# Two of the projections' tile pairs go from direct products to seven-product slots, and the mixer's pieces are placed anew

## The reference

```python
xn   = rmsnorm(x, norm1_g)
q, k, v, r, a_lr, cb, cc, ch, cu, cv = split(xn @ w_in)    # 512, 512, 1024, 1024, 16, then five of 512
loga = log_sigmoid(a_lr @ w_a2 + b_a) / 16
o, S = gla_chunked(q, k, v, loga, S0)                      # gated linear attention, chunks of 64
o_gla  = rmsnorm_per_head(o) * gla_g * silu(r)
o_conv = cb * (conv_b + sum_j conv_w[j] * shifted(cc * ch, j))
vv     = layernorm(gelu(cv));  o_cm = gelu(cu) * (Wm @ vv + cm_bs)     # ChunkMLP, chunks of 128
h = x + concat[o_gla, o_conv, o_cm] @ w_out
y = rmsnorm(h + swiglu(rmsnorm(h, norm2_g)), final_g)
```

## Time and profile before

| | before |
|---|---|
| three runs | 2188.55, 2187.94, 2188.02 us; median 2188.02 |
| the profiled execution's own time | 2187.62 us |
| its span in the trace | 2185.9 us |
| PE busy | 2173.7 us, 99%, 17352 matmuls |
| DVE, ACT, POOL busy | 1714.6 (78%), 1003.4 (46%), 9.0 us (0%) |
| granted TensorE clock, mean | 0.997 |

### The profile page before, as it was taken

One profiled execution on the slowest core, in us unless ns is written; L12 is line 12 of the kernel. 1 busy time (PEld: TensorE's weight loads), 2 busy tenths in 40 slices (PEclk: granted clock), 3 DMA queues, 4 the chain that ended last, 5 costly groups with the idle time before them and its releaser, 6 DMA issues.

```text
span 2185.9 us, 40925 instructions
## 1 busy us (share of the span) xinstructions
PE 2173.7 (99%) x17352; PEld 2168.9 (99%) x17352; DVE 1714.6 (78%) x1994; ACT 1003.4 (46%) x1331; POOL 9.0 (0%) x14
## 2 busy tenths in 40 slices
PE   9999999999999999999999999999999999999998
PEld 9999999999999999999999999999999999999998
DVE  7765478446796789888888887888888888787887
ACT  7433523124454455444444544444444545444455
POOL 0000000000000000000000000000000000000000
PEclk9999999999999999999999999999999999999998
DMA  5332324245333435344445445434545876555523
GB/s 191 95 109 89 106 69 146 80 143 195 110 107 106 149 116 166 123 150 160 141 141 158 145 128 165 152 124 146 163 141 174 302 279 225 181 208 190 188 84 115
DMA packets 121583, 325.63 MB, mean 149 GB/s; under 512 B 10702, under 2 KB 51214, under 8 KB 120432
## 3 DMA queue, kind: packets, MB, share of 16 engines
q1 hardware_dynamic: 120928, 323.82, 44.0%
q10 hardware_dynamic: 528, 0.07, 0.0%
HBM read 267.22 MB, written 56.63 MB: 148 GB/s over the span
## 4 chain that ended last, share of the span: by engine, by line
PE 97%; DVE 1%; issue 1%; ACT 1%; POOL 0%; POOLq 0%; DVEq 0%; ACTq 0%
PE acc L1622 24%; PE acc L1307 21%; PE g L1622 18%; PE acc L1630 12%; PE g L1630 9%; PE acc L1531 2%; PE acc L1569 2%; PE g L1531 2%; PE g L1569 2%; PE g L1523 1%; PE acc L1523 1%; PE g L1334 0%; PE g L1457 0%; PE g L1326 0%; PE g L1464 0%
## 5 line engine op out<-in xcount | busy, mean ns | idle before, releaser
L1128 ACT CAST w_hi<-w_s 128x1024 fp32r<-128x1024 f32 (+1 forms) x204 | 209.1, 1025 | 357.1 <-DVE w_s L2438 351.0
L1622 PE MATMUL g<-op_hi,w_hi 128*128 128x272 f32 x1056 | 272.1, 288 | 0.0
L1622 PE MATMUL acc<-op_hi,w_hi 128*128 128x272 f32 x1056 | 271.7, 288 | 0.4 <-ACT acc L1102 0.4
L1622 PE MATMUL g<-op_lo,w_hi 128*128 128x272 f32 x1056 | 271.9, 288 | 0.0
L1622 PE MATMUL acc<-sg_hi,w_hi 128*128 128x272 f32 x1056 | 271.8, 288 | 0.0
L1622 PE MATMUL acc<-op_lo,w_hi 128*128 128x272 f32 x1056 | 271.4, 288 | 0.0
L1622 PE MATMUL acc<-sg_lo,w_hi 128*128 128x272 f32 x1056 | 271.4, 288 | 0.0
L1307 PE MATMUL acc<-op_hi,w_hi 128*128 128x272 f32 x1280 | 267.6, 290 | 0.0
L1307 PE MATMUL acc<-op_hi,w_lo 128*128 128x272 f32 x1280 | 264.8, 288 | 0.0
L1307 PE MATMUL acc<-op_lo,w_hi 128*128 128x272 f32 x1280 | 264.7, 288 | 0.0
L2413 DVE TENSOR_TENSOR w_lo<-w_s,w_hi 128x1024 fp32r<-128x1024 f32 (+1 forms) x204 | 242.7, 1190 | 12.4 <-ACT w_hi L1128 6.4
(11 more groups left out here) (396 smaller groups left out, 4676.8 us busy)
## 6 DMA issues: line engine op xcount, KB each, us to landing
w<-w_gu SPq DMA_DIRECT2D x88, 512.0 KB, 3.3
w_raw<-w_gu SPq DMA_DIRECT2D x88, 512.0 KB, 3.9
w_raw<-w_in SPq DMA_DIRECT2D x64, 512.0 KB, 3.6
hf_dram<-hf_hi SPq DMA_DIRECT2D x22, 952.0 KB, 6.4
hf_dram<-hf_lo SPq DMA_DIRECT2D x22, 952.0 KB, 8.7
w_raw<-w_d SPq DMA_DIRECT2D x32, 512.0 KB, 4.3
w<-w_d SPq DMA_DIRECT2D x26, 512.0 KB, 3.2
op_hi<-hf_dram SPq DMA_DIRECT2D x16, 544.0 KB, 7.0
```

Of the source, the lines that this page charges most:

```text
L1128: nc.scalar.copy(w_hi[:, (C_ST + n) % RING, 0:w], src[:, 0:w]).then_inc(hi_ready, 1)
L1622: nc.tensor.matmul(out, w_h, x, start=fresh and j == 0 and i == 0, stop=False, skip_group_check=True)
```

## The change

Four of r's eight tiles (those of the attention's `mix` tiles 4 to 7) leave the stage of half tiles. Their columns of w_in go in front of those of k and v, and are made in two slots more (`NR = 2`, `NQ = 8`), with seven products each, ahead of k. Their outputs lie in `trunk` 12 to 15 until SP stores them to `r_dram` (two stores of 0.56 MB), since v needs the place. Late in the stage they are read back (one DMA of 1.11 MB), ACT takes their Silu at `C_T` + 37, and DVE multiplies them into `mix` at the next chunk.

The stage has 48 half tiles instead of 56, and all pieces are placed anew. From `C_T`: vt 0, 1, 2; z 3, 6; b 5, 7, 9, 11, 13; kdt 15; qs 17 to 24; mu 18; var_cm 20; s 22, 25, 27, 29, 31, 32, 33, 35, 36, 37; vvt 25; zc 26, 27; p 28, 30, 32, 34; on 35, 37, 39, 41. The heads are normed in the order 2, 3, 0, 1. w_out's seven-product half now takes `mix` tiles 4 to 11, and its direct half 12 to 15 and 0 to 3. The square root and DVE's reciprocal in the answers to var_cm and on become Ln and Exp(-0.5 ·) on ACT. The reload of x for tiles 12 to 15 moves to the stage's last chunk.

```diff
-T_Q, T_CV, T_CONV, T_CU, T_R, N_IN = 1, 17, 21, 33, 37, 45
+T_Q, T_CV, T_CONV, T_CU, T_R, N_IN = 1, 17, 21, 33, 37, 41
-NQ = 6
+NR = 2
+NQ = NR + 6
-MIX_ORDER = list(range(HK, KT)) + list(range(HK))
+MIX_ORDER = list(range(4, 12)) + list(range(12, KT)) + list(range(4))
+HEAD_ORDER = (2, 3, 0, 1)
-B_AT = tuple(C_T + 8 + 2 * i for i in range(5))
-KDT_AT = C_T + 18
-QS_AT = tuple(C_T + 20 + i for i in range(8))
-MU_AT, VAR_CM_AT, VVT_AT, ZC_AT = C_T + 19, C_T + 21, C_T + 28, (C_T + 30, C_T + 32)
-S_AT = (C_T + 25, C_T + 29, C_T + 32) + tuple(C_T + 33 + 2 * i for i in range(7))
-P_AT = tuple(C_T + 34 + 2 * i for i in range(4))
-OSQ_AT = C_T + 40
-ON_AT = tuple(C_T + 42 + 2 * i for i in range(4))
+B_AT = tuple(C_T + 5 + 2 * i for i in range(5))
+KDT_AT = C_T + 15
+QS_AT = tuple(C_T + 17 + i for i in range(8))
+MU_AT, VAR_CM_AT, VVT_AT, ZC_AT = C_T + 18, C_T + 20, C_T + 25, (C_T + 26, C_T + 27)
+S_AT = tuple(C_T + i for i in (22, 25, 27, 29, 31, 32, 33, 35, 36, 37))
+P_AT = tuple(C_T + 28 + 2 * i for i in range(4))
+OSQ_AT = C_T + 34
+ON_AT = tuple(C_T + 35 + 2 * i for i in range(4))
+R_AT = C_T + 37
...
+        def slot_out(s):
+            return kv[:, s + 4 if s < NR else s - NR]
...
             for s in range(1, NQ):
                 for j in (1, 3, 0, 4, 2):
                     load_kv_block(s, j)
+                if 2 <= s < NR + 2:
+                    sp.wait_ge(kv_out, s - 1)
+                    sp.wait_ge(kv_read, 4 * (s - 1))
+                    sp.dma_start(r_dram[:, 2 * (s - 2):2 * (s - 1), :], slot_out(s - 2)).then_inc(r_out, 16)
...
-                if c == C_T + 10:
+                if c == C_T + 13:
                     sp.wait_ge(inter, number(("z", 1)))
                     load_s0(0)
                     load_s0(1)
...
-                    for i in range(4):
+                    for i in range(3):
                         sp.dma_start(trunk[:, 4 * i:4 * i + 4, :], xT[:, 4 * i:4 * i + 4, :]).then_inc(x_back, 16)
+                if c == P_AT[-1] + 8:
+                    sp.wait_ge(inter, number(("p", PAIRS - 1)))
+                    sp.wait_ge(r_out, 16 * NR)
+                    sp.dma_start(trunk[:, KT - 2 * NR:, :], r_dram).then_inc(r_in, 16)
+                if c == C_OUT - 1:
+                    sp.wait_ge(front_done, 2 * NR)
+                    sp.dma_start(trunk[:, 12:, :], xT[:, 12:, :]).then_inc(x_back, 16)
...
-                    last = nc.scalar.activation(two(orstd), g01[:, :, 0:TH], ACT.Sqrt, bias=EPS, scale=1.0 / DV)
+                    chain(nc.scalar.activation(two(orstd), g01[:, :, 0:TH], ACT.Ln, bias=EPS, scale=1.0 / DV))
+                    last = nc.scalar.activation(orstd, orstd, ACT.Exp, scale=-0.5)
...
                 split_hi(c + 4, c + 4)
+                if c == R_AT:
+                    act.wait_ge(r_in, 16)
+                    for i in range(2 * NR):
+                        nc.scalar.activation(trunk[:, KT - 2 * NR + i, :], trunk[:, KT - 2 * NR + i, :], ACT.Silu)\
+                            .then_inc(r_act, 1)
...
-                    chain(nc.vector.reciprocal(orstd, orstd))
                     if i < 3:
                         out_square_sum(i + 1)
                     for e in range(2):
-                        m = 2 * i + e
+                        m = 2 * HEAD_ORDER[i] + e
...
                 split_lo(c + 4, c + 4)
+                if c == R_AT + 1:
+                    dve.wait_ge(post_v, parts(V_KINDS, ("on", 1)))
+                    for i in range(2 * NR):
+                        dve.wait_ge(r_act, i + 1)
+                        nc.vector.tensor_tensor(mix[:, 4 + i, :], mix[:, 4 + i, :], trunk[:, KT - 2 * NR + i, :],
+                                                ALU.mult).then_inc(front_done, 1)
...
-    kv = np.concatenate([wk, wv], axis=1)
+    kv = np.concatenate([wr[:, (KT // 2 - 2 * NR) * P:], wk, wv], axis=1)
```

More of the change, by code:

```diff
@@ L268, in build @@
         form_lo = (sg_lo[:, 0], opf_lo[:, 0], opf_lo[:, 1], sg_lo[:, 1], opf_lo[:, 2], sg_lo[:, 2], opf_lo[:, 3])
-        mg = mxf[:, HK * T:].rearrange("p (i b t) -> p i b t", i=HP, b=4)
+        mg = mxf[:, 4 * T:12 * T].rearrange("p (i b t) -> p i b t", i=HP, b=4)
         ta_hi, ta_lo = ([o[:, f // 2, HP * (f % 2):HP * (f % 2) + HP] for f in range(4)] for o in (opf_hi, opf_lo))
@@ L272, in build @@
         mixform_lo = (fa_lo[:, 0], ta_lo[0], ta_lo[1], fa_lo[:, 1], ta_lo[2], fa_lo[:, 2], ta_lo[3])
-        kv = trunk[:, 4:KT, :].rearrange("p (s m) t -> p s m t", s=NQ)
+        kv = trunk[:, 4:KT, :].rearrange("p (s m) t -> p s m t", s=NQ - NR)
         y_out = [[y[:, f, 0:HP, :] for f in range(4)] for y in (y_first, y_second)]
         aside = hid.rearrange("p (q r) t -> p q r t", q=2)
+        r_dram = nc.dram_tensor("r_dram", (P, 2 * NR, T), F32).ap()
         h_dram = nc.dram_tensor("h_dram", (P, KT, T), F32).ap()
@@ L325, in build @@
         x_back = sem("x_back")
+        r_out = sem("r_out")
+        r_in = sem("r_in")
+        r_act = sem("r_act")
+        front_done = sem("front_done")
         wa_in = sem("wa_in")
@@ L672, in _ @@
             spill_h(7)
-            sp.wait_ge(mix_done, 8)
+            sp.wait_ge(mix_done, 4)
             sp.dma_start(conv_o, cst[:]).then_inc(stored, 16)
@@ L843, in out_squares @@
                 for e in range(2):
-                    nc.scalar.activation(osq[:, e, :], mix[:, 2 * h + e, :], ACT.Square).then_inc(osq_a, 1)
+                    nc.scalar.activation(osq[:, e, :], mix[:, 2 * HEAD_ORDER[h] + e, :], ACT.Square).then_inc(osq_a, 1)
             def post(kind, i):
@@ L882, in post @@
                 elif kind == "var_cm":
-                    last = nc.scalar.activation(two(lnb[:]), g23[:, :, 0:TH], ACT.Sqrt, bias=EPS, scale=1.0 / (4 * P))
+                    chain(nc.scalar.activation(two(lnb[:]), g23[:, :, 0:TH], ACT.Ln, bias=EPS, scale=1.0 / (4 * P)))
+                    last = nc.scalar.activation(lnb[:], lnb[:], ACT.Exp, scale=-0.5)
                 elif kind == "vvt":
@@ L913, in op_hi_tile @@
             def op_hi_tile(k):
-                act.wait_ge(mix_done, k + 1)
+                act.wait_ge(mix_done, k - 3)
                 act.wait_ge(chunk_done, C_OUT)
@@ L918, in mix_single_hi @@
             def mix_single_hi():
-                act.wait_ge(mix_done, 8)
+                act.wait_ge(mix_done, 4)
+                act.wait_ge(front_done, 2 * NR)
                 act.wait_ge(post_v, parts(V_KINDS, order[-1]))
@@ L951, in mix_block_hi @@
                     else:
-                        act.wait_ge(mix_done, KT)
+                        act.wait_ge(mix_done, KT - 2 * NR)
                     nc.scalar.copy(aside[:, :, 1, :], pc[:, :, 0:TH]).then_inc(p5_aside, 1)
@@ L1980, in post @@
                     dve.wait_ge(post_a, parts(A_KINDS, (kind, i)))
-                    chain(nc.vector.reciprocal(lnb[:], lnb[:]))
                     for h in range(4):
@@ L2184, in kv_outputs @@
             def kv_outputs(s, piece):
-                q, y = s % 2, kv[:, s]
+                q, y = s % 2, slot_out(s)
                 dve.wait_ge(chunk_done, done_q(NPQ * s + (5, 5, 6, 7)[piece]))
                 if piece == C11:
+                    if s >= NR + 4:
+                        dve.wait_ge(r_out, 16 * (s - NR - 3))
                     nc.vector.tensor_tensor(y[:, 0, 0:TH], pa[:, q, 0:TH], rstd[:, 0:TH], ALU.mult).then_inc(kv_read, 1)
@@ L2746 @@
     conv = np.concatenate([y[:, i * P:(i + 1) * P] for i in range(4) for y in (wcc, wch, wcb)], axis=1)
-    win = tiles(np.concatenate([wq, wcv, conv, wcu, wr], axis=1))
+    win = tiles(np.concatenate([wq, wcv, conv, wcu, wr[:, :(KT // 2 - 2 * NR) * P]], axis=1))
     wo = a["w_out"][0].reshape(KT, P, D)[MIX_ORDER].reshape(D, D)
```

## The result

The changed kernel took 2207.94 us in the median of five runs (2205.84 to 2210.51), against 2187.98 of the kernel before in runs beside it (2187.76 to 2188.55). The ratio is 1.0091, with a 95% interval of 1.008 to 1.0102. It is slower by 20 us, where 11.4 were forecast. The profiled execution took 2205.84 us, the fastest of the five, so its trace has 18.2 us to explain, and the median has 2 more.

The account below looks back on a forecast made before the run. PE's in-order queue was taken to bound the kernel from end to end. Waits of 16.3 us, less an old wait of 0.3 and saved work of 4.6, gave +11.4: 2199.0 profiled, 2199.4 median; range 2194.5 to 2206.

Parts of the forecast that it names:

- Work saved, 4.6 us: PE's matmul work: eight half tiles go (48.16 us), two seven-product slots come (43.54), saving 4.6 us.
- The waits of the stage, 1 to 7: PE waits at z1 3.8, mu 0.9, s1 2.0, p1 0.9, s5 2.0, on0 3.6, on3 0.8 us.
- z1's: Wait 1: PE waits ahead of z1 for DVE's and ACT's answer to b0, 3.8 us.
- 6: Wait 6: on0 behind s7 in one half tile, PE waits for DVE's updates, 3.6 us.
- Wait 8, w_out's start, 2.3 us: PE waits at w_out's first products because DVE builds their forms 2.4 us later than before; 2.3 us.
- PE's clock falls in the waits: Rival: granted clock halves after long waits, 2.7 us per fall; 2202.1 for one, 2204.8 for two; chance 0.22.
- the two longest waits: Waits 1 and 6: z1 behind b0, 3.8 us, and on0 behind s7, 3.6 us.
- the rival's 2204.8: Clock rival's time in us if the clock falls in both of the two longest waits; rival's chance 0.22.
- DMA lateness: Rival: S0's first loads or r's read-back late, lateness beyond 15 us paid one for one; 2203 and over; chance 0.06.
- one load for Ln and Exp: Rival: ACT's answers to `on` are one 1.28 us table load shorter; 2197.5 us; chance 0.08.
- hidden answers: Rival: answers reach PE in time, only saved work shows; 2183.4 us; chances 0.04 faster, 0.05 same.
- these eight waits: Forecast waits 1 to 7 in the stage and 8 at w_out's start, 16.3 us in sum.

Follow-up runs that it names:

- the last kernel: Changed kernel with all freed waits, pieces moved earlier, ACT answering on1 to on3 before the Silu, x reloads behind late weight blocks; 2183.01 us, ratio 0.9977 to the kernel before.
- the kernel with four long waits: The changed kernel itself, with the waits at z1, s1, s5 and on0; 2207.94 us, ratio 1.0091 to the kernel before.
- the two with one: Kernel before with b0 ahead of z1, 2192.88 us; changed kernel with z1, on0, mu, p1 and s5 waits freed, 2195.68 us.
- the one with everything freed: Changed kernel with freed waits, x reloads spread, and kdt, qs, mu, var_cm, s0, vvt one half tile earlier; 2188.91 us, ratio 1.0004 to the kernel before.

## Why the prediction was wrong

- *Work saved, 4.6 us*: right. It is the 43.6 and 48.0 of the account to within 0.2, and what the last kernel gains.
- *The waits of the stage, 1 to 7*: right, each within 0.4 us, 13.8 for 14.0 in sum. (By its own rows, 6 is 3.5 and not 3.6.) z1's, freed alone, was paid back in full, and of the 9.9 us of five freed together 1.4 came back as a new wait and 0.6 at w_out.
- *Wait 8, w_out's start, 2.3 us*: mis-sized; it is 3.4 by the list and 3.9 by the starts. The bound for it reached only from zero to 1 us more. The mechanism (forms late by DVE's and ACT's queues behind on3) was right: with the on answer ahead of the Silu 2.3 us of it go, and with the stage's other lateness too, all of it. Spreading the reloads of x alone gave nothing; with ACT's new order the block behind them does hold ACT, for 5.2 us, and how much moving them to the end adds in the last kernel wasn't tried by itself.
- *"PE's clock falls in the waits", 0.22*: this is the step that failed. It wasn't a rival to the count but a part of it. I priced a fall at 2.7 us and allowed it in the two longest waits; a stretch at 0.50 costs 1.53, but it comes behind the waits of 2.0 and 1.8 us too. The profiled execution lost 4.6 us so, behind z1, s1 and s5. That the rival's 2204.8 lies within 1.1 of the profiled 2205.84 is partly luck: two falls at 2.7 are nearly as much as three at 1.53, and behind on0, one of the two that it named, the clock didn't fall in this execution. The granted clock of its five runs (0.993 to 0.995, the slowest run at 0.993) against 0.997 for the kernel before puts the median's further 2 us there as well; the trace of a slower run isn't at hand, so that is argued and not shown. The scatter speaks for it, though not alone: 4.7 us over the five runs of the kernel with four long waits, 1.6 and 2.1 in the two with one, 0.8 over ten runs in the last kernel with none; but 2.9 in the one with everything freed, whose waits in the stage and in w_out are of 1.6 us at most.
- *DMA lateness, one load for Ln and Exp, hidden answers*: none of the three happened in the changed kernel; no wait of PE's list ends with a DMA.
- Forecast of +11.4 and found +18.2 in the profile, 6.8 more: 4.6 are the clock, 1.6 w_out's start, and 0.6 small differences of the other terms. The direction and the place were right, the range ended 2 us too low.

## What to carry to other kernels

When the busiest engine runs in order and is fed by answers, compressing the schedule is not free even if every engine has room: write down, for each pair of neighbouring pieces, what the second really waits for. Five of these eight waits weren't asked for by the data: one was for a bank where another was free, four were for answers that the piece, or its first matmuls, didn't use. The cure was another bank, a shorter list, another order in the half tile, or a wait moved behind the matmuls that don't need it. With them freed, a few pieces moved, ACT's order turned round and the reloads of x put at the end, a change that lost 20 us gains 5. Price a stall of TensorE of 2 us and more at its length plus a part of the clock's fall, and read the windows behind every such wait, and the scatter of the runs.

## What the runs showed of the hardware

In eight profiles (the changed kernel and seven experiments) there were 24 waits of PE of 1.8 to 3.4 us inside dense work, and behind 17 of them the granted clock was 0.50 in the record: at z1 4 of 4, s1 6 of 7, on0 4 of 6, s5 2 of 6, and the one of 3.1 us at w_out's start. None followed the 36 shorter waits there, whose matmuls start 0.8 to 2.0 us apart. Nowhere else between the kernel's first 7 us and its last 13 was it 0.50, in these profiles or in the four without such waits. The stretch was 3.4 us long in 12 cases and 6.8 in 5. The same wait of the same length could do either: behind on0's 3.4 us it stayed at 1.00 in the changed kernel and in one other, and fell in four. In each of the six profiles that have both s5's and on0's wait, 28 us apart, it fell behind exactly one of the two; why, no run shows. The 128x272 matmuls of such a stretch start 0.227 us apart instead of 0.125, 1.8 times as long and not twice, so that 3.4 us of it cost 1.5 us and not half its length; the five of 6.8 us cost 2.4 to 3.1. The Trainium skill, "TensorE: Matmul & The Clock Gate", in the section "What's actually happening", has half the clock as the state that follows an idle stretch; these profiles agree, with 17 of 24.
